# First expert's rows and last expert's sum by one-hot products, and the three passes of each product in another order

## Chip, cores and metric

One core of a Trainium2 chip runs the kernel. The metric is the device time of one launch in microseconds. The median of three runs is 1960.74 us.

## What is computed

Two layers of a decoder trunk on 256 tokens of width 1024, all in float32. The reference, cut to its frame:

```python
for l in range(2):
    h = rmsnorm(x, norm_mix[l])
    ... = split(h @ w_in[l])                      # 5316 columns: three token mixers, and gates
    merged = g0 * (o_a @ w_pa[l]) + g1 * (o_b @ w_pb[l]) + g2 * (o_c @ w_pc[l])
    x = x + merged @ w_out[l]
    x = x + cross_attention(rmsnorm(x), rmsnorm(mem), w_xq[l], w_xkv[l], w_xo[l], ...)
    hf = rmsnorm(x, norm_ffn[l])
    x = x + (swiglu(hf, ...) if l == 0 else moe_swiglu(hf, ...))

def moe_swiglu(t, w_router, w_gu, w_down):        # 8 experts, 1024 -> 2 x 3584 -> 1024
    top_val, top_idx = top_k(t @ w_router, 2)
    gate = sum(one_hot(top_idx) * softmax(top_val))
    return sum(gate[:, e] * swiglu(t, w_gu[e], w_down[e]) for e in range(8))
```

## The kernel before

**Products in three passes.** Every float32 product but those of the gates and the attention is split: the weights w and the activations h each into a rounded high part and a rest, and the product is h_hi w_hi + h_lo w_hi + h_hi w_lo. A weight tile is 1 MB (128 partitions x 2048 floats) in one of three slots `raw`. ACT copies it to `w_hi` (`act_split`, L383; in the expert stage L820), DVE subtracts to get `w_lo` (`dve_split`, L388; L884). Semaphores `hi_done` and `lo_done` count them. Three slots of `w_hi` and `w_lo` go round: the fourth split waits until PE is through with the first (`mm_done`). For the activations ACT writes `hT_hi` (`act_hi`, L490, semaphores such as `mix_H`), DVE `hT_lo` (`dve_lo`, L495, `mix_L`). `pe_products` (L499) runs over the row blocks k of a slot and does all three passes for one k before the next:

```python
pe.matmul(acc, a, wh, start=start and j == 0, stop=False)     # L504
pe.matmul(acc, b, wh, start=False, stop=False)                # L505
ins = pe.matmul(acc, a, wl, start=False, stop=stop and last)  # L506
```

It is called by `pe_block_slot` (L509) for the linears, by `pe_dense` for the dense layer and by `pe_moe_gate_up` and `pe_moe_down` for the experts; each first waits for `lo_done` of its slot and for the low part of the activations. The order of work on each engine is written out by hand, engine by engine. A linear has slots of 4 row blocks x 512 columns, "pa" and "pb" of 2 x 512. Layer by layer come xkv ("mem" is its input), in ("mix"), the mixers, pa, pb, pc, out ("mrg"), xq ("x"), cross attention, xo, and the feed-forward part ("ffn").

**The expert stage.** `dve_router` (L1551) takes the logits, finds the two best experts per token, and PE counts the ranks of the tokens in each expert (L1203 to L1207). From them DVE computes `row_no`, the row that each of a token's two copies has in a list in DRAM, `expert_rows`: 128 rows per expert (L1584), and `n_iter`, the number of blocks of 128 rows, 8 here. DVE normalises x into `xn` (L1683). POOL scatters `xn` into the list by four indirect DMAs (L318), waits for them, and loads block 0 (L321). PE turns the block (`pe_turn_rows`, L754: 8 transposes), ACT and DVE split it (L832, L898), and expert 0 begins. Inside each expert POOL loads the next block, PE turns it after the third chunk, and ACT's output copy `y_sb` of the expert before (L836) is put back in the list by POOL (L329).

An expert is 14 chunks of 256 hidden columns, 3 weight tiles each: two for gate and up (`pe_moe_gate_up`), one for the way down (`pe_moe_down`), the last one for the chunk before. Between the two, PE turns the product silu(gate) * up of the chunk before (L716); ACT makes its high part `aT_hi` (L828), DVE the low one, `aT_lo` (L893, `aT_split`). SP loads tiles six ahead, as DVE frees them. `pe_moe`, `act_moe` and `dve_moe` run expert 0 and 1 apart, then a loop over pairs, whose count each engine reads into a register.

**The end.** The last down product has no chunk around it. ACT: silu, the split of the last tile, `aT_hi`, then the copy of the output (L876 to L880); DVE the same. Then POOL puts the block in DRAM, waits, gathers each token's two rows by four indirect DMAs into `yg` (L335), and DVE adds them to x, times the gates (L937). SP stores each half of the tokens.

## Time and profile before

| | |
|---|---|
| median of three runs | 1960.74 us (1956.84 to 1961.72) |
| the profiled execution: its time, its span | 1955.1 us, 1953.5 us |
| mean granted clock of PE | 0.96 |
| PE busy | 1754.0 us, 90% |
| DVE busy | 1377.2 us, 70% |
| ACT busy | 1059.5 us, 54% |
| POOL busy | 49.8 us, 3% |
| read from HBM | 483.55 MB, 257 GB/s over the span |

Times in the profile are counted from the span's start. PE is the matmul engine, and its busy time is not a measure of its peak; PEld is its weight load. Work is in two halves: up to 950 us the two layers with their mixers, each engine with pauses, and from 953 us on the expert stage.

### The profile page before, as it was taken

How to read it: one execution, taken by the hardware profiler on the slowest of the kernel's cores; microseconds unless marked ns; L12 is line 12 of the kernel's file. 1: busy time of each engine (PE TensorE's matmuls, PEld its weight loads, DVE VectorE, ACT ScalarE, POOL GpSimd, SP SyncE). 2: the span in 40 equal slices, each digit the busy share in tenths (PEclk: the TensorE clock that was granted, in tenths of full speed). 3: DMA queues.
4: the chain of work that ended last, by engine and by line, in shares of the span. 5: the costliest groups of instructions: out<-in, count | busy, mean ns of one | idle time of the engine just before them, and what ended most of it. 6: DMA issues, size and time to landing. Idle time of an engine off the chain costs nothing.

```text
span 1953.5 us, 21775 instructions
## 1 busy us (share of the span) xinstructions
PE 1754.0 (90%) x7553; PEld 1348.9 (69%) x7553; DVE 1377.2 (70%) x1288; ACT 1059.5 (54%) x967; POOL 49.8 (3%) x69
## 2 busy tenths in 40 slices
PE   6796878799989968886499999999999999999995
PEld 5653466688867634665388887888888888888884
DVE  6447467554456464674488888888888888888884
ACT  4212434434343224243377777777777777777773
POOL 2100000000000000000100000000000000000000
PEclk9898989899989989897799999999999999999997
DMA  8821259255435312440699999999999999999993
GB/s 240 266 91 63 82 194 363 103 194 190 175 127 175 109 66 82 178 177 22 233 355 370 376 367 371 371 371 373 367 376 369 366 381 365 376 368 365 382 363 137
DMA packets 74813, 502.80 MB, mean 257 GB/s; under 512 B 8524, under 2 KB 9356, under 8 KB 18320
## 3 DMA queue, kind: packets, MB, share of 16 engines
q1 hardware_dynamic: 65712, 466.55, 62.6%
q0 software_dynamic: 8656, 34.57, 5.7%
q10 hardware_dynamic: 400, 1.08, 0.1%
q8 instruction: 28, 0.46, 0.1%
q14 instruction: 17, 0.14, 0.0%
HBM read 483.55 MB, written 18.61 MB: 257 GB/s over the span
## 4 chain that ended last, share of the span: by engine, by line
PE 76%; DVE 10%; ACT 6%; DMA 3%; issue 2%; DVEq 2%; POOL 0%; ACTq 0%; SPq 0%; POOLq 0%
PE ps L504 23%; PE ps L505 23%; PE ps L506 23%; DMA raw<-in_layer_tiles 3%; PE ps L569 2%; DVE w_lo L388 2%; PE ps L716 1%; ACT scratch L1259 1%; ACT w_hi L383 1%; DVE scratch L1386 1%; DVE st L1357 1%; DVEq L1360 1%; DVE scratch L1436 1%; DVE st L1440 1%; DVE hT_lo L495 1%
## 5 line engine op out<-in xcount | busy, mean ns | idle before, releaser
L504 PE MATMUL ps<-w_hi,hT_hi 128*128 128x512 f32 x1488 | 610.6, 410 | 57.9 <-DVE hT_lo L495 24.1
L505 PE MATMUL ps<-w_hi,hT_lo 128*128 128x512 f32 x1488 | 597.3, 401 | 0.0
L506 PE MATMUL ps<-w_lo,hT_hi 128*128 128x512 f32 x1488 | 596.6, 401 | 0.0
L884 DVE TENSOR_TENSOR w_lo<-raw,w_hi 128x2048 fp32r<-128x2048 f32 x168 | 385.0, 2292 | 69.4 <-ACT w_hi L820 69.4
L884 DVE TENSOR_TENSOR w_lo<-z,w_hi 128x2048 fp32r<-128x2048 f32 x168 | 384.5, 2290 | 51.7 <-ACT w_hi L820 48.6
L504 PEld LDWEIGHTS ps<-w_hi,hT_hi 128*128 128x128 f32 x1488 | 285.1, 192 | 130.4 <-DVE w_lo L388 30.0
L820 ACT ACTIVATE w_hi<-z 128x2048 fp32r<-128x2048 f32 x168 | 321.6, 1915 | 40.6 <-PE ps L506 34.7
L820 ACT ACTIVATE w_hi<-raw 128x2048 fp32r<-128x2048 f32 x168 | 321.0, 1911 | 24.3 <-PE ps L506 24.3
L506 PEld LDWEIGHTS ps<-w_lo,hT_hi 128*128 128x128 f32 x1488 | 285.3, 192 | 68.9
L505 PEld LDWEIGHTS ps<-w_hi,hT_lo 128*128 128x128 f32 x1488 | 285.6, 192 | 62.4
L388 DVE TENSOR_TENSOR w_lo<-raw,w_hi 128x2048 fp32r<-128x2048 f32 (+1 forms) x89 | 194.6, 2194 | 126.9 <-ACT w_hi L383 126.2
L383 ACT ACTIVATE w_hi<-raw 128x2048 fp32r<-128x2048 f32 (+1 forms) x89 | 162.6, 1834 | 199.7 <-PE ps L506 128.9
L504 PE MATMUL ps<-w_hi,aT_hi 128*128 128x512 f32 x536 | 213.6, 398 | 3.5 <-DVE aT_lo L893 2.0
L506 PE MATMUL ps<-w_lo,aT_hi 128*128 128x512 f32 x536 | 212.7, 397 | 0.0
L505 PE MATMUL ps<-w_hi,aT_lo 128*128 128x512 f32 x536 | 212.7, 397 | 0.0
L569 PE MATMUL ps<-raw 128*128 128x512 f32 (+1 forms) x384 | 158.4, 570 | 26.4 <-DVE z L579 26.4
L569 PEld LDWEIGHTS ps<-raw 128*128 128x128 f32 x384 | 72.7, 197 | 107.5 <-issue 107.2
L504 PEld LDWEIGHTS ps<-w_hi,aT_hi 128*128 128x128 f32 x536 | 100.9, 188 | 31.4 <-issue 5.5
L506 PEld LDWEIGHTS ps<-w_lo,aT_hi 128*128 128x128 f32 x536 | 101.1, 189 | 24.5
L505 PEld LDWEIGHTS ps<-w_hi,aT_lo 128*128 128x128 f32 x536 | 101.0, 188 | 23.7
L828 ACT ACTIVATE aT_hi<-ps 128x256 fp32r<-128x256 f32 x112 | 43.2, 385 | 107.9 <-PE ps L716 107.9
L824 ACT ACTIVATE headsT<-ps 128x256 f32<-128x256 f32 x112 | 42.9, 383 | 65.4 <-PE ps L506 65.4
(235 smaller groups left out, 1015.8 us busy)
## 6 DMA issues: line engine op xcount, KB each, us to landing
z<-in_moe_tiles SPq DMA_DIRECT2D x168, 1024.0 KB, 4.9
raw<-in_moe_tiles SPq DMA_DIRECT2D x168, 1024.0 KB, 4.8
raw<-in_layer_tiles SPq DMA_DIRECT2D x68, 1024.0 KB, 4.9
raw<-in_dense_tiles SPq DMA_DIRECT2D x33, 1024.0 KB, 4.8
rows_of_experts<-z POOLq DMA_DIRECT2D x1, 8704.0 KB, 44.2
z<-in_b_gate POOLq DMA_DIRECT2D x4, 1536.0 KB, 11.4
z<-rows_of_experts POOLq DMA_DIRECT2D x9, 512.0 KB, 8.2
raw<-in_layer_tiles SPq DMA_DIRECT2D x8, 512.0 KB, 3.9
```

What stands on the lines that cost most here:

```text
L383: act.activation(w_hi[:, ring, 0:width], raw[:, ring, 0:width], ACT.Copy).then_inc(sem("hi_done"), 1)
L388: v.tensor_tensor(w_lo[:, ring, 0:width], raw[:, ring, 0:width], w_hi[:, ring, 0:width].bitcast(F32), ALU.subtract).then_inc(sem("lo_done" ...
L495: v.tensor_tensor(hT_lo[:, ks, :], src[:, ks, :], hT_hi[:, ks, :].bitcast(F32), ALU.subtract) \
L504: pe.matmul(acc, a, wh, start=start and j == 0, stop=False)
L505: pe.matmul(acc, b, wh, start=False, stop=False)
L506: ins = pe.matmul(acc, a, wl, start=False, stop=stop and last)
L569: ins = pe.matmul(ps[:, LIN + i, 0:n], gate_x(l)[:, kk, i * P:(i + 1) * P], w[:, k, :], start=kk == 0, stop=kk == KC - 1)
L716: ins = pe.transpose(ps[:, 6, f * P:(f + 1) * P], a_sb[:, 0, f * P:(f + 1) * P], ident)
L820: act.activation(w_hi[:, ring, :], moe_raw(p), ACT.Copy).then_inc(sem("hi_done"), 1)
L824: act.activation(silu_sb[:, 0, :], ps[:, bank, 0:FC], ACT.Silu).then_inc(sem("silu"), 1)
L828: act.activation(aT_hi[:, :, 0:P], psA(1), ACT.Copy).then_inc(sem("aT_hi"), 1)
L884: v.tensor_tensor(w_lo[:, ring, :], moe_raw(p), w_hi[:, ring, :].bitcast(F32), ALU.subtract) \
```

## The change

1. `pe_products` does the high-high matmuls of all row blocks first, then the low-high ones, then high-low. The wait before it asks for the high parts (`hi_done`, `..._H`, `aT_hi`); those for the low part of the activations (`x_lo`) and of the weights (`w_lo_v`) stand between the passes, for the first column tile of a slot.
2. The first block is not read back from DRAM. DVE makes `first_hot`, 128 tokens x 128 rows, from the smaller of a token's two row numbers, and PE multiplies `xn` by it (L803 of the new file), which gives the turned rows at once. `xn` is x times the gain, made by DVE before the router, then scaled by ACT. The scatter of all rows stays.
3. The last block's output is not put in DRAM. `dve_last` makes `last_hot` between the second and third expert, PE turns it, ACT copies it. At the end PE multiplies `y_sb` by it, half by half, and DVE adds the result to x times the gate. The rows of the other experts are gathered during the last expert, and POOL scales and adds them. The list's padding block is loaded only after the last put has landed.
4. At the end, the split of the last tile stands ahead of the last silu, and the output is stored in quarters.

The diff, cut:

```diff
+            for n in range(2 * TT):
+                h, i = n // TT, n % TT
+                sp.wait_ge(sem("x_final"), n + 1)
+                sp.dma_start(out[0, i * P:(i + 1) * P, h * NB:(h + 1) * NB], x_sb[:, i, h * NB:(h + 1) * NB]) \
+                    .then_inc(sem("stored"), 16)
+            sp.wait_ge(sem("stored"), 16 * 2 * TT)
...
-            load_rows(pool, 0)
             pool.wait_ge(sem("routed"), 1)
             n_it = pool.value_load(n_iter[0:1, 0:1], min_val=N_EXP, max_val=2 * N_EXP)
-            def turn_rows(m, done):
+            with pool.Fori(1, n_it) as m:
 
                 pool.wait_ge(sem("rows_T"), m)
                 load_rows(pool, m)
                 pool.wait_ge(sem("y_sb"), m)
-                pool.dma_start(expert_rows[bass.ds(m * P - P, P), :], y_sb).then_inc(sem(done), 16)
-            with pool.Fori(1, n_it) as m:
-                turn_rows(m, "rows_put")
-            turn_rows(n_it, "last_put")
-            pool.wait_ge(sem("last_put"), 16)
+                pool.dma_start(expert_rows[bass.ds(m * P - P, P), :], y_sb).then_inc(sem("rows_put"), 16)
+            pool.wait_ge(sem("rows_T"), n_it)
+            pool.wait_ge(sem("rows_put"), n_it * 16)
+            load_rows(pool, n_it)
+
             for k in range(2 * TT):
                 pool.indirect_dma_start(yg[:, k, :], None, expert_rows, bass.IndirectOffsetOnAxis(row_no[:, k:k + 1], 0)) \
                     .then_inc(sem(f"y_back{k}"), 16)
+            pool.wait_ge(sem("g_split"), 1)
+            for k in range(2 * TT):
+                j, i = k // TT, k % TT
+                pool.wait_ge(sem(f"y_back{k}"), 16)
+                if j:
+                    pool.wait_ge(sem("x_part"), i + 1)
+                pool.tensor_scalar(yg[:, k, :], yg[:, k, :], g_other[:, j, i:i + 1], None, ALU.mult)
+                pool.drain()
+                pool.tensor_tensor(x_sb[:, i, :], x_sb[:, i, :], yg[:, k, :], ALU.add).then_inc(sem("x_part"), 1)
...
-        def pe_products(pe, acc, hk, wk, start, stop, hi=hT_hi, lo=hT_lo):
-
-            for j, ((k, cols), (wh, wl)) in enumerate(zip(hk, wk)):
-                a, b = hi[:, k, cols], lo[:, k, cols]
-                last = j == len(hk) - 1
-                pe.matmul(acc, a, wh, start=start and j == 0, stop=False)
-                pe.matmul(acc, b, wh, start=False, stop=False)
-                ins = pe.matmul(acc, a, wl, start=False, stop=stop and last)
+        def pe_products(pe, acc, hk, wk, start, stop, hi=hT_hi, lo=hT_lo, x_lo=None, w_lo_v=None):
+
+            for j, ((k, cols), (wh, _)) in enumerate(zip(hk, wk)):
+                pe.matmul(acc, hi[:, k, cols], wh, start=start and j == 0, stop=False)
+            if x_lo is not None:
+                pe.wait_ge(sem(x_lo[0]), x_lo[1])
+            for (k, cols), (wh, _) in zip(hk, wk):
+                pe.matmul(acc, lo[:, k, cols], wh, start=False, stop=False)
+            if w_lo_v is not None:
+                pe.wait_ge(sem("lo_done"), w_lo_v)
+            for j, ((k, cols), (_, wl)) in enumerate(zip(hk, wk)):
+                ins = pe.matmul(acc, hi[:, k, cols], wl, start=False, stop=stop and j == len(hk) - 1)
             return ins
 
-        def pe_block_slot(pe, ring, kcs, n, k0, lo_v, first, final, blk_v):
-
-            pe.wait_ge(sem("lo_done"), lo_v)
+        def pe_block_slot(pe, ring, kcs, n, k0, lo_v, first, final, blk_v, x_lo=None):
+
+            pe.wait_ge(sem("hi_done"), lo_v)
...
+                                  x_lo=x_lo if i == 0 else None, w_lo_v=lo_v if i == 0 else None)
...
+                    x_lo = None
                     if h_ready and b == b0:
-                        pe.wait_ge(sem(h_ready), 2 * l + h + 1)
-                    pe_block_slot(pe, place[ss_], kcs, n, k0 + 4 * h, split_no(ss_) + 1, h == 0, h == per - 1, evs)
+                        pe.wait_ge(sem(h_ready + "_H"), 2 * l + h + 1)
+                        x_lo = (h_ready + "_L", 2 * l + h + 1)
...
-                pe.wait_ge(sem("aT_split"), c + 1)
+                pe.wait_ge(sem("hi_done"), s + (1 - N_GATE))
+                pe.wait_ge(sem("aT_hi"), c + 1)
...
-            pe_turn_rows(pe, 0)
+            pe.wait_ge(sem("first_hot"), 1)
+            pe.wait_ge(sem("xn_rows"), 1)
+            for k in range(KC):
+                for i in range(TT):
+                    ins = pe.matmul(psG[:, k, :], xn[:, i, k * P:(k + 1) * P], first_hot[:, i, :],
+                                    start=i == 0, stop=i == TT - 1)
+            ins.then_inc(sem("rows_T"), 1)
             for par in range(2):
                 pe_expert(pe, 0, par)
+            pe.wait_ge(sem("last_hot"), 1)
+            for i in range(TT):
+                ins = pe.transpose(ps[:, 7, i * P:(i + 1) * P], last_hot[:, i, :], ident)
+            ins.then_inc(sem("last_T"), 1)
...
+            lo_v, aT_v = n_pair * (2 * MOE) + SPL0, n_pair * (2 * N_MOE) + N_DENSE
+            pe.wait_ge(sem("hi_done"), lo_v)
+            pe.wait_ge(sem("aT_hi"), aT_v)
...
+                pe_products(pe, ps[:, h, :], [(f, slice(0, P)) for f in range(2)],
+                            [(wh[:, f, cols], wl[:, f, cols]) for f in range(2)], False, True, hi=aT_hi, lo=aT_lo,
+                            x_lo=("aT_split", aT_v) if h == 0 else None, w_lo_v=lo_v if h == 0 else None) \
+                    .then_inc(sem("last_y"), 1)
+            pe.wait_ge(sem("last_to_token"), 1)
+            for h in range(2):
+                pe.wait_ge(sem("last_y_sb"), h + 1)
+                for i in range(TT):
+                    pe.matmul(ps[:, LAST[h][i], :], last_to_token[:, i * P:(i + 1) * P], y_sb[:, h * NB:(h + 1) * NB],
+                              start=True, stop=True).then_inc(sem("spread"), 1)
...
+            act.wait_ge(sem("top_two"), 1)
+            act.activation(g2[:, 0:2], g2[:, 0:2], ACT.Exp).then_inc(sem("gate_exp"), 1)
+            act.wait_ge(sem("last_T"), 1)
+            act.activation(last_to_token, ps[:, 7, 0:2 * P], ACT.Copy).then_inc(sem("last_to_token"), 1)
             act.wait_ge(sem("routed"), 1)
             n_pair = act.value_load(n_iter[0:1, 1:2], min_val=N_EXP // 2, max_val=N_EXP)
             with act.Fori(1, n_pair) as ip:
                 for par in range(2):
                     act_expert(act, ip, par)
+            act_moe_split(act, 2, moe_ring(0), n_pair * (MOE // 3 * 16), n_pair * (2 * MOE) + (MOE0 - 3))
...
             act_silu(act, 5, n_pair * (2 * MOE) + (MOE0 - 2))
-            act_moe_split(act, 2, moe_ring(0), n_pair * (MOE // 3 * 16), n_pair * (2 * MOE) + (MOE0 - 3))
...
-            act_y(act, n_pair * (2 * MOE) + MOE0)
+            for h in range(2):
+                act.wait_ge(sem("last_y"), h + 1)
+                act.activation(y_sb[:, h * NB:(h + 1) * NB], ps[:, h, :], ACT.Copy).then_inc(sem("last_y_sb"), 1)
...
+            dve_last(v)
...
+            dve_moe_split(v, 2, moe_ring(0), n_pair * (2 * MOE) + SPL0)
             dve_gated(v, 5, n_pair * (2 * N_MOE) + N_DENSE)
-            dve_moe_split(v, 2, moe_ring(0), n_pair * (2 * MOE) + SPL0)
...
-                for j in range(2):
-                    v.wait_ge(sem(f"y_back{j * TT + i}"), 16)
-                    ins = v.scalar_tensor_tensor(x_sb[:, i, :], yg[:, j * TT + i, :], g2[:, 4 + 2 * j + i:5 + 2 * j + i],
-                                                 x_sb[:, i, :], ALU.mult, ALU.add)
-                    v.drain()
-                v.drain().then_inc(sem("x_final"), 1)
+            v.wait_ge(sem("x_part"), 2 * TT)
+            for n in range(2 * TT):
+                h, i = n // TT, n % TT
+                dst = x_sb[:, i, h * NB:(h + 1) * NB]
+                v.wait_ge(sem("spread"), n + 1)
+                v.scalar_tensor_tensor(dst, ps[:, LAST[h][i], :], slot[:, i:i + 1], dst, ALU.mult, ALU.add) \
+                    .then_inc(sem("x_final"), 1)
...
+                    act.wait_ge(sem("ffn_rs"), l + 1)
+                    for i in range(TT):
+                        ins = act.activation(xn[:, i, :], xn[:, i, :], ACT.Copy, scale=norm_rs[:, 6 + i:7 + i])
+                    ins.then_inc(sem("xn_rows"), 1)
...
+            dve_newton(v, "ffn", L - 1, norm_rs[:, 6:8]).then_inc(sem("ffn_rs"), 1)
...
+            v.tensor_tensor(slot, row_f[:, 0, :], row_f[:, 1, :], ALU.min)
+            v.drain()
+            for i in range(TT):
+                ins = v.tensor_scalar(first_hot[:, i, :], iota, slot[:, i:i + 1], None, ALU.is_equal)
+            ins.then_inc(sem("first_hot"), 1)
...
+        def dve_last(v):
+
+            v.tensor_scalar(last0, n_f[:, 2:3], float(P), -float(P), ALU.mult, ALU.add)
+            v.drain()
+            v.tensor_scalar(from_last, row_f, last0, None, ALU.subtract)
+            v.drain()
+            v.tensor_tensor(slot, from_last[:, 0, :], from_last[:, 1, :], ALU.max)
+            v.tensor_scalar(in_last, from_last, 0.0, None, ALU.is_ge)
+            v.drain()
+            for i in range(TT):
+                ins = v.tensor_scalar(last_hot[:, i, :], iota, slot[:, i:i + 1], None, ALU.is_equal)
+            ins.then_inc(sem("last_hot"), 1)
...
+            v.tensor_tensor(g_last, g, in_last, ALU.mult)
+            v.drain()
+            v.tensor_tensor(g_other, g, g_last, ALU.subtract).then_inc(sem("g_split"), 1)
+            v.tensor_tensor(slot, g_last[:, 0, :], g_last[:, 1, :], ALU.add)
...
-                    dve_newton(v, "ffn", l, norm_rs[:, 6:8])
-                    v.drain()
                     v.wait_ge(sem("gain_row"), 16)
                     for i in range(TT):
-                        ins = v.scalar_tensor_tensor(xn[:, i, :], x_sb[:, i, :], norm_rs[:, 6 + i:7 + i], gain_row,
-                                                     ALU.mult, ALU.mult)
-                    ins.then_inc(sem("xn_rows"), 1)
+                        v.tensor_tensor(xn[:, i, :], x_sb[:, i, :], gain_row, ALU.mult)
```

`pe_moe_down`, `pe_moe_gate_up` and the functions of `pe_dense` take the new waits in the same way as `pe_block_slot`.

**Place 1: PE, the down product of a chunk in the expert loop.** `aT_hi`, `aT_lo` are the turned activations, and the waits are semaphores. Before:

```order
L504 MATMUL ps<-w_hi,aT_hi 128x512 [waits aT_split,lo_done]
L505 MATMUL ps<-w_hi,aT_lo 128x512
L506 MATMUL ps<-w_lo,aT_hi 128x512
L504 MATMUL ps<-w_hi,aT_hi 128x512
L505 MATMUL ps<-w_hi,aT_lo 128x512
L506 MATMUL ps<-w_lo,aT_hi 128x512
L504 MATMUL ps<-w_hi,aT_hi 128x512
L505 MATMUL ps<-w_hi,aT_lo 128x512
L506 MATMUL ps<-w_lo,aT_hi 128x512
```

After the change:

```order
L512 MATMUL ps<-w_hi,aT_hi 128x512 [waits aT_hi,hi_done]
L512 MATMUL ps<-w_hi,aT_hi 128x512
L516 MATMUL ps<-w_hi,aT_lo 128x512 [waits aT_split]
L516 MATMUL ps<-w_hi,aT_lo 128x512
L520 MATMUL ps<-w_lo,aT_hi 128x512 [waits lo_done]
L520 MATMUL ps<-w_lo,aT_hi 128x512
L512 MATMUL ps<-w_hi,aT_hi 128x512 x2
L516 MATMUL ps<-w_hi,aT_lo 128x512 x2
L520 MATMUL ps<-w_lo,aT_hi 128x512 x2
```

Matmuls of one pass now stand together, two in each half of the columns, where the three passes alternated; the waits for the two low parts have moved behind two and four matmuls.

**Place 2: ACT, from the last turn of the second expert to the first split of the third.** L865 (before: L820) is the copy to `w_hi`, L873 (L828) `aT_hi`. Before:

```order
L828 ACTIVATE aT_hi<-ps 128x2x128 [waits aT_turned]
L813 REGISTER_ALU
L813 COMPARE_AND_BRANCH
L872 TENSOR_LOAD n_iter [waits routed]
L872 ISA x2
L873 UNCONDITIONAL_BRANCH
L873 ISA
L819 ISA [waits moe_full0]
L820 ACTIVATE w_hi<-z 128x2048 [waits mm_done]
```

After:

```order
L873 ACTIVATE aT_hi<-ps 128x2x128 [waits aT_turned]
L858 REGISTER_ALU
L858 COMPARE_AND_BRANCH
L917 ACT_TABLE_LOAD
L917 ACTIVATE headsT<-headsT 128x2 [waits top_two]
L919 ACTIVATE scratch<-ps 128x256 [waits last_T]
L921 TENSOR_LOAD n_iter [waits routed]
L921 ISA x2
L922 UNCONDITIONAL_BRANCH
L922 ISA
L864 ISA [waits moe_full0]
L865 ACT_TABLE_LOAD
```

Between them stand the exponential of the gates with its table, and a copy of what PE turns at `last_T`. On PE these two turns stand behind the last down product of the second expert:

```order
L520 MATMUL ps<-w_lo,aT_hi 128x512 x2
L794 REGISTER_ALU
L794 COMPARE_AND_BRANCH
L810 MATMUL ps<-consts,scratch 128x128 [waits last_hot]
L810 MATMUL ps<-consts,scratch 128x128
L813 TENSOR_LOAD n_iter [waits routed]
L813 ISA x2
```

Before, nothing of ACT's stood there but the register's load.

**Place 3: ACT at the end.** Before:

```order
L823 ISA
L824 ACTIVATE headsT<-ps 128x256 [waits mm_done]
L818 REGISTER_ALU
L819 REGISTER_ALU [waits moe_full2]
L820 ACTIVATE w_hi<-z 128x2048 [waits mm_done]
L827 ISA
L828 ACTIVATE aT_hi<-ps 128x2x128 [waits aT_turned]
```

After:

```order
L863 REGISTER_ALU
L864 ISA [waits moe_full2]
L865 ACTIVATE w_hi<-z 128x2048 [waits mm_done]
L868 REGISTER_ALU
L869 ACTIVATE headsT<-ps 128x256 [waits mm_done]
L872 ISA
L873 ACTIVATE aT_hi<-ps 128x2x128 [waits aT_turned]
```

The split of the last tile (`moe_full2`) has moved ahead of the silu (L869, before L824).

## Rows read from the trace of the kernel before

**Rows 1.** Windows, expert stage: us, busy by engine, clock of PE, DMA share, GB/s.

```profile
1100.00:1400.00 300.00, 300.00 (x1335) 241.10 (x1334) 262.62 (x177) 222.79 (x177) 2.13 (x4) 1.00 0.96 371
```

**Rows 2.** Timeline (start, duration), PE from one tile to the next.

```profile
1900.37 0.40 PE L506 MATMUL ps<-w_lo,aT_hi 128*128 128x512 f32 x1
1900.37 0.19 PEld L504 LDWEIGHTS ps<-w_hi,hT_hi 128*128 128x128 f32 x1
1900.61 0.40 PE L504 MATMUL ps<-w_hi,hT_hi 128*128 128x512 f32 x1
```

**Rows 3.** Waits of PE: total us, times, longest.

```profile
PE ps L504 <- DVE hT_lo L495: 24.1, 11, 3.6
...
PE ps L504 <- DVE w_lo L388: 8.5, 4, 2.2
...
PE ps L504 <- DVE w_lo L884: 1.6, 1, 1.6
```

**Rows 4.** Timeline, the start of the first expert; in brackets idle before, releaser.

```profile
917.71 2.48 DVE L1683 SCALAR_TENSOR_TENSOR scratch<-x_sb,st,z 128x1024 f32<-128x1024 f32 x2
...
925.72 0.17 DVE L1584 CAST row_no<-headsT 128x4 uint32<-128x4 f32 x1
...
945.18 0.59 POOL L310 DMA_DIRECT2D z<-rows_of_experts  x1 [10.71 <-DMA rows_of_experts<-scratch,row_no]
...
948.68 1.97 PE L758 MATMUL ps<-consts,z 128*128 128x128 f32 x8 [24.08 <-DMA z<-rows_of_experts]
950.69 1.02 ACT L832 ACTIVATE hT_hi<-ps 128x1024 fp32r<-128x1024 f32 x1 [24.23 <-PE ps L758]
...
951.74 1.22 DVE L898 TENSOR_TENSOR hT_lo<-ps,hT_hi 128x1024 fp32r<-128x1024 f32 x1 [19.36 <-ACT hT_hi L832]
...
953.02 0.80 PE L504 MATMUL ps<-w_hi,hT_hi 128*128 128x512 f32 x1 [2.37 <-DVE hT_lo L898]
```

**Rows 5.** Timeline, the end.

```profile
1926.04 2.29 DVE L884 TENSOR_TENSOR w_lo<-z,w_hi 128x2048 fp32r<-128x2048 f32 x1 [1.38 <-ACT w_hi L820]
...
1926.42 0.38 PE L716 MATMUL ps<-consts,headsT 128*128 128x128 f32 x2
...
1928.82 0.48 PE L504 MATMUL ps<-w_hi,aT_hi 128*128 128x512 f32 x1 [2.01 <-DVE aT_lo L893]
...
1933.44 1.02 ACT L836 ACTIVATE z<-ps 128x1024 f32<-128x1024 f32 x1 [6.22 <-PE ps L506]
...
1947.73 2.64 DVE L937 SCALAR_TENSOR_TENSOR x_sb<-scratch,headsT,x_sb 128x1024 f32<-128x1024 f32 x2 [0.17 <-issue]
```

**Rows 6.** Timeline, PE in "pa" of the first layer.

```profile
257.17 0.69 PE L504 MATMUL ps<-w_hi,hT_hi 128*128 128x512 f32 x1 [2.10 <-DVE w_lo L388]
257.66 0.63 PE L505 MATMUL ps<-w_hi,hT_lo 128*128 128x512 f32 x1
258.08 0.63 PE L506 MATMUL ps<-w_lo,hT_hi 128*128 128x512 f32 x1
```

**Rows 7.** Timeline, PE with whole float32 operands.

```profile
163.62 1.06 PE L1060 MATMUL ps<-scratch,consts 128*128 128x128 f32 x4
...
190.85 3.70 PE L569 MATMUL ps<-raw 128*128 128x512 f32 x8
```

**Rows 8.** Timeline, ACT's table load; ACT and PE from second to third expert.

```profile
953.53 1.28 ACT L824 ACT_TABLE_LOAD   x1
...
1192.62 1.92 ACT L820 ACTIVATE w_hi<-z 128x2048 fp32r<-128x2048 f32 x1 [0.78 <-issue]
...
1196.91 0.50 PE L504 MATMUL ps<-w_hi,hT_hi 128*128 128x512 f32 x1
```

**Rows 9.** DMA issues: count, KB each, us from issue to landing, in the expert stage.

```profile
rows_of_experts<-z POOLq DMA_DIRECT2D x2, 512.0 KB, 6.7
z<-rows_of_experts POOLq DMA_DIRECT2D x2, 512.0 KB, 8.2
```

**Rows 10.** Timeline, POOL in the first layer.

```profile
288.24 3.84 POOL L281 MEMSET z<- 128x4488 f32 x1 [152.47 <-DVE scratch L1487]
```

90 lines of the change are left out of this document (50 added, 40 removed).

## The prediction

> **What bounds the kernel now.** I read four views: the windows, the waits of PE, the timeline of the three places that the change touches, and the groups by line. The profiled execution took 1955.1 us, 5.6 us under the median of the runs (1960.74); all sums are made against it, and the difference is carried over to the median at the end.
>
> Half of the span, from 953 us on, is the expert stage: 8 experts, 14 chunks each, 3 weight tiles a chunk. There PE is never idle: 300 us of a 300 us window [rows 1]. Its products follow each other every 0.233 us, also from the last of one weight tile to the first of the next, which has a wait before it [rows 2]. A chunk of 36 products and two turns (the transposes, about 0.11 us each) takes 8.61 us. Here only fewer or faster products would help, and the change has the same number. DVE and ACT have 12% and 26% idle in it, DMA is at 0.96.
>
> What can be won lies outside. Of the first half the reader should see the waits of PE for the low part of an operand [rows 3], and two holes: the start of the first expert, where PE stands for 24.1 us until the rows come back from DRAM [rows 4], and the end, where nothing but one expert's output is written out, gathered and added [rows 5].
>
> **Part 1, high-high passes first.** Each product of a slot now asks for the high parts alone, does its high-high matmuls, then waits for the low part of the activations, then for that of the weights. PE reaches the wait with 4 matmuls done (2 where the slot has 2 row blocks, and 8 where the weights are the late part). The pause itself stays, so each such wait gives at most the matmuls put ahead of it: 4 x 0.233 = 0.93 us at the high clock, 4 x 0.427 = 1.7 at the low one [rows 6], and about DVE's own part at most, 1.22 us for 1024 columns [rows 4] and 2.29 for 2048 [rows 5].
> - activations of "mem", two layers, at the low clock, where DVE still makes the weights' low half as well: 2 x 1.7 = 3.4
> - "mix", two layers: 0.9 and 1.2; "out" and "x", two layers: 4 x 0.93; "ffn" 0.93: 6.8. With "mem" these are the waits for hT_lo, 24.1 us in 11 waits, two of which (the start of "xo") keep theirs.
> - the four waits for w_lo in "pa" and "pb", 8.5 us together [rows 3], with 2 high-high and 2 low-high matmuls ahead each: 4 x 1.0 = 4.0
> - the end of the dense layer, aT_lo, 2 matmuls: 0.5.
>
> That is 14.7 us. In the expert stage one wait is left, 1.6 us for w_lo in the first chunk [rows 3]; 8 matmuls (1.87 us) now cover it: 1.6.
> The clock: after a wait of 2.1 us eight matmuls come 0.427 us apart [rows 6], so PE is at the lower of its two levels (1.2 GHz); each such stretch costs 8 x 0.194 = 1.6 us. Nine such stretches stand behind a wait that becomes shorter or is broken in two. None need go (0), all may (14). I take 4, nearer the low end: waits of about 2 us have a fall behind them [rows 5, 6], and no row here tells how short is short enough. Part 1 in all: 20.3.
>
> **Part 2, the first expert's rows from SBUF.** Before [rows 4] the two normalising operations end and the router begins at 920.1, row numbers are there at 925.9, the expert's first matmul is at 953.0. Now those two (2.48 us from 917.71) leave the path: DVE multiplies x by the gain alone, from 914.2 on, and the router starts at 916.9, when the logits land. That is 3.2 us earlier: row arithmetic ends at 922.5, plus a minimum and two 128-column comparisons, about 0.7: 923.2. ACT has scaled the rows by then (Newton steps 920.0, two of 1.05: 922.0). PE does 16 fp32 matmuls of 128 columns. Four of these took 1.06 us at the low clock with the last one's tail [rows 7], 0.215 each: 16 x 0.215 = 3.4, and 0.3 until ACT sees them: 926.9. ACT makes the high part in 1.02 [rows 4], and PE starts at 928.0 with 4 matmuls; DVE, which has two weight splits first (to 928.5), adds the low part by 929.7. So the start moves from 953.0 to 928.0: **25.0**. The four row scatters and the second expert's load now run beside the first chunks: the scatters had landed 19.3 us after the row numbers (the load of 945.18), so now near 943, the load near 950, and PE asks for these rows after 8 tiles, at 953. Costed at nothing; if that cover is gone PE stands for the difference.
>
> **Part 3, the end.** Before [rows 5]: turn 1926.4, last down product starts 1928.8, since ACT's silu stood ahead of its last split and DVE's too; PE ends at 1933.4, half of it at the low clock; then ACT's copy, the store, the gather, four additions until 1950.4, the output stored by 1953.5. Now the split runs in the idle of ACT from 1921.4 (it needs a slot that PE freed at 1920.7): high part 1923.4, low 1925.7, gated product 1926.1, in time for the turn. PE starts at 1927.3 on aT_hi, 12 x 0.233: 1930.1. The gap is 0.6 us in place of 2.0, so I expect the high clock to hold. The first half of y is copied meanwhile (0.6). Four fp32 matmuls of 512 columns, 0.46 each (eight in 3.70 [rows 7]): 1931.9, and DVE adds four halves of 0.75 behind them: 1933.7. With the same 3.1 us from last addition to end: 1936.8, a gain of **16.7**; at the low clock from 1929 on it would be 13.5.
>
> **What it costs.** (a) Between the second and third expert ACT now waits for PE: the exponential of the gates with its table load (1.28 [rows 8]), then "last_T", two turns that PE does after the last down product. Before, ACT had made the next tile's high part by then: it began at 1192.62 and was done 2.4 us before PE wanted it at 1196.91 [rows 8]. Now: PE free at 1196.85, turns seen 0.4 later, copy 0.38, register load 0.78, a table load again 1.28, split 1.92: PE stands until 1201.6, 4.5 us. The low halves then come from DVE one after another (2.29 each, three and two short ones before aT_lo), while PE wants aT_lo after 24.5 matmuls: another 2. Together -6.5. The loop's two further table loads per pair of experts hide in ACT's idle quarter; if that is gone, 1.5 us for each of 3 pairs.
> (b) In the last expert POOL waits for the seventh expert's put to land before it loads the padding block that PE still turns: put at 10.1 us into the expert, 6.7 to land, then 8.2 [rows 9]: 25.5, when PE wants it at 25.9. The gather of 2 MB follows at once. Bounds 0 and 8; I take -1.5, near the lower end, since tiles are asked for six ahead.
> (c) POOL's eight operations on 128x1024, and DVE's 15 small ones between experts two and three (inside the stall of (a)): 0.5.
>
> Sum: 20.3 + 25.0 + 16.7 - 6.5 - 2.0 = **53.5**. Own time 1901.6; carried to the median, 1907.
>
> **A rule against this change.** The nearest row for POOL's arithmetic is the clearing of z, 4488 columns in 3.84 us [rows 10], so 0.88 us for 1024 with one input, and I double it for two: 4 x (0.88 + 1.76) = 10.6 us. No two-input DVE operation ran from SBUF beside it, so what it does to DVE is not in the trace; bounds are 0 and the 10.6 whole.
> The Trainium skill, page "GPSIMD Engine Reference", section "Key points", says that POOL shares its SBUF interfaces with VectorE and contends with DVE instructions that have two SBUF inputs. w_lo is exactly such an instruction.
>
> **Rivals.**
> 1. POOL holds DVE up. All 10.6 us stand in DVE's way; its 12% idle over some 30 us takes 3.6, and PE waits 7: 1914. This is the page's rule as named above. 12%.
> 2. The early start starves. The rows of expert two, or tiles behind the scatters, come later than PE asks, with PE standing 5 to 12 us and its clock falling: 1907 + 10 = 1917. For: DMA at 0.96 in the stage. Against: 6 tiles lie ready, and the first 8 take PE 24 us. 12%.
> 3. The clock gives more: all low stretches go, and (a) costs 4: 1907 - 10 - 2.5 = 1894. 12%.
> 4. Slower than before: the new wait in the middle of a product keeps PE from loading the next weights ahead. Place: the wait for lo_done before the third pass, 336 tiles in the expert stage alone. Price: one exposed load, 0.19 us each [rows 2], 64 us: 1971. It decides from 0.16 us per tile. Against: the waits that stand at each tile's start now cost 0.00 [rows 2]. 3%.
> 5. The change does less than it says: the first-pass matmuls just move a wait, nothing downstream comes earlier since the loads of weight tiles set the pace; part 1 gives 5: 1922. 6%.
>
> **How the numbers follow.** Forecast 55%: 1907, with its own bounds 1900 to 1915. The range takes in rivals 1, 2 and part of 3 and 5: 1896 to 1922. A measurement tells 0.3% (6 us) from no change. Only rival 4 is no gain: faster 0.96, same 0.01, slower 0.03.
>
> **What would show it.** L512 replaces L504 in PE's waits with the same pauses, now split over L512, L516 and L520, about 15 us less in total. First L512 of the first expert 25 us plus part 1 earlier, and no L779 wait in front of it. A wait of 4 to 5 us of PE for ACT w_hi at the third expert, once. From PE's last down product to the end 7 to 8 us in place of 20.1. Wrong if the chunk in the expert stage is not 8.61 us any more (rival 4), if DVE's w_lo lengthens beside POOL (rival 1), or if PE waits for DMA at L779 (rival 2).

## The result, and the profile after

The changed kernel took 1916.48 us (median of 4 runs, 1909.52 to 1917.71) beside 1961.23 for the kernel before on the same chip: ratio 0.977 [0.974, 0.979], 44.8 us less where 53.5 were forecast. The time lies in the range, 9.5 us above 1907. The profiled execution has a span of 1914.1 us, 39.4 less than that of before. In the four later measurements of this document the kernel before had medians of 1955.0 to 1956.9 us, near its profiled execution (1955.1), so 1961.23 may lie some 5 us high and 39.4 may be the better size of the gain. From the page of the profile:

```profile
span 1914.1 us, 21886 instructions
PE 1762.0 (92%) x7587; PEld 1350.6 (71%) x7587; DVE 1384.1 (72%) x1300; ACT 1070.5 (56%) x978; POOL 82.9 (4%) x75
```

The waits of PE (total us, times, longest), which answer to [rows 3]:

```profile
PE ps L512 <- DVE z L596: 13.1, 3, 11.4
...
PE ps L512 <- ACT hT_hi L500: 8.8, 9, 1.8
...
PE ps L516 <- DVE aT_lo L944: 5.3, 7, 1.7
...
PE ps L512 <- ACT w_hi L865: 4.3, 1, 4.3
...
PE ps L520 <- DVE w_lo L398: 3.0, 4, 1.2
PE ps L512 <- DVE hT_lo L505: 2.8, 2, 1.4
...
PE ps L779 <- DMA z<-rows_of_experts: 2.6, 1, 2.6
...
PE ps L512 <- ACT w_hi L393: 1.6, 3, 0.7
```

The waits for the parts of operands fell: hT_lo from 24.1 us to 2.8 here and 1.3 in L516, with 8.8 for hT_hi in its place, and w_lo from 8.5 to 3.0, with 1.3 of the 1.6 for w_hi in its place, 15.4 in all. Other waits ahead of the router grew by part of that: "z" by 2.7, evacuations into scratch ahead of L512 by 2.3, x_sb by 1.9; others fell. The stretch up to the router, first before, then after (the second number is its length, then PE's time at work; 0.95 is the granted clock):

```profile
0.00:912.80 912.80, 768.96 (x3183) 556.49 (x3184) 511.54 (x677) 328.78 (x384) 30.11 (x44) 0.95 0.45 155
```
```profile
0.00:900.08 900.08, 769.34 (x3184) 552.45 (x3184) 511.13 (x676) 328.70 (x384) 30.17 (x44) 0.95 0.45 157
```

So PE stands 143.8 us before the router in the old kernel and 130.7 in the new one, 13.1 less, and its time at work is 769.0 and 769.3. Three waits of the expert stage are new or have grown: 5.3 us for aT_lo, 4.3 for w_hi and 2.6 for the padding rows, where PE had stood for nothing over long stretches [rows 1].

The timeline of PE from router to first product, which answers to [rows 4]:

```profile
900.08 3.71 PE L1260 MATMUL ps<-w_router,scratch 128*128 128x8 f32 x32 [0.20 <-ACT scratch L1395]
...
910.29 5.67 PE L803 MATMUL ps<-scratch 128*128 128x128 f32 x32 [1.89 <-DVE scratch L1650]
917.08 1.20 PE L512 MATMUL ps<-w_hi,hT_hi 128*128 128x512 f32 x4 [1.11 <-ACT hT_hi L877]
```

The router starts 12.7 us earlier (912.80 before), the first product 35.9 earlier: 12.7 from part 1, 23.2 from part 2. The end, which answers to [rows 5]:

```profile
1903.39 0.38 PE L735 MATMUL ps<-consts,headsT 128*128 128x128 f32 x2
1904.34 0.70 PE L512 MATMUL ps<-w_hi,aT_hi 128*128 128x512 f32 x2 [0.57 <-ACT aT_hi L873]
...
1907.20 3.59 PE L835 MATMUL ps<-z,scratch 128*128 128x512 f32 x8
1908.34 3.25 DVE L991 SCALAR_TENSOR_TENSOR x_sb<-ps,headsT,x_sb 128x512 f32<-128x512 f32 x4 [3.69 <-PE ps L835]
```

From the start of the last down product to the end it is 9.7 us (24.7 before), and the gap ahead of it 0.57 in place of 2.01.

Between the first product and the last down product the stage grew from 975.8 to 987.3 us. To see where, read one turn (L735, L716 before) to the next. Before, a chunk is 8.61 us, and 9.49 where the rows of the next expert are turned. Now four places differ:

| turns | before | after | more |
|---|---|---|---|
| start of the third expert (27th and 28th) | 8.78, 8.63 | 14.94, 9.13 | 6.7 |
| end of a pair of experts, twice | 8.61 | 9.28 | 1.4 |
| padding rows turned (at 1793.7) | 9.49 | 13.57 | 4.1 |
| three chunks from 1824.5 on | 8.61 | 10.58, 9.74, 9.67 | 4.2 |

### The profile page after: what moved, and what is told of

It reads as the page before. It is cut to its first block, busy times and chain, and to the rows that moved or that the text cites. A ratio compares the mean times of both kernels' runs of the same rounds, so it can differ in the third digit from the quotient of the medians.

```text
span 1914.1 us, 21886 instructions
## 1 busy us (share of the span) xinstructions
PE 1762.0 (92%) x7587; PEld 1350.6 (71%) x7587; DVE 1384.1 (72%) x1300; ACT 1070.5 (56%) x978; POOL 82.9 (4%) x75
## 4 chain that ended last, share of the span: by engine, by line
PE 73%; DVE 11%; ACT 7%; DMA 4%; issue 3%; DVEq 2%; ACTq 0%; SPq 0%; POOLq 0%
PE ps L516 22%; PE ps L520 22%; PE ps L512 22%; DMA raw<-in_layer_tiles 3%; DVE w_lo L398 2%; PE ps L586 2%; DVE w_lo L935 1%; ACT w_hi L393 1%; PE ps L735 1%; ACT scratch L1321 1%; DVE scratch L1450 1%; DVE st L1421 1%; ACT w_hi L865 1%; DVEq L1424 1%; DVE scratch L1500 1%
## 5 line engine op out<-in xcount | busy, mean ns | idle before, releaser
L512 PE MATMUL ps<-w_hi,hT_hi 128*128 128x512 f32 x1488 | 427.2, 408 | 45.2 <-DVE z L596 13.1
L935 DVE TENSOR_TENSOR w_lo<-raw,w_hi 128x2048 fp32r<-128x2048 f32 x168 | 391.1, 2329 | 64.3 <-ACT w_hi L865 64.3
L516 PE MATMUL ps<-w_hi,hT_lo 128*128 128x512 f32 x1488 | 414.8, 400 | 1.8 <-DVE hT_lo L505 1.3
L520 PE MATMUL ps<-w_lo,hT_hi 128*128 128x512 f32 x1488 | 412.7, 399 | 3.0 <-DVE w_lo L398 3.0
L512 PEld LDWEIGHTS ps<-w_hi,hT_hi 128*128 128x128 f32 x1488 | 271.7, 191 | 108.5 <-issue 22.7
L865 ACT ACTIVATE w_hi<-z 128x2048 fp32r<-128x2048 f32 x168 | 321.3, 1915 | 40.7 <-PE ps L520 35.9
L865 ACT ACTIVATE w_hi<-raw 128x2048 fp32r<-128x2048 f32 x168 | 320.9, 1911 | 25.5 <-PE ps L520 25.5
L516 PEld LDWEIGHTS ps<-w_hi,hT_lo 128*128 128x128 f32 x1488 | 282.6, 190 | 73.5 <-DVE hT_lo L505 5.2
L586 PE MATMUL ps<-raw 128*128 128x512 f32 (+1 forms) x384 | 162.0, 581 | 28.1 <-DVE z L596 28.1
L516 PE MATMUL ps<-w_hi,aT_lo 128*128 128x512 f32 x536 | 169.2, 397 | 5.3 <-DVE aT_lo L944 5.3
L512 PE MATMUL ps<-w_hi,aT_hi 128*128 128x512 f32 x536 | 168.5, 396 | 1.3 <-ACT aT_hi L702 0.8
L520 PE MATMUL ps<-w_lo,aT_hi 128*128 128x512 f32 x536 | 168.4, 396 | 0.0
L586 PEld LDWEIGHTS ps<-raw 128*128 128x128 f32 x384 | 74.0, 200 | 111.6 <-issue 111.4
L516 PEld LDWEIGHTS ps<-w_hi,aT_lo 128*128 128x128 f32 x536 | 100.1, 188 | 32.4 <-DVE aT_lo L944 8.3
L512 PEld LDWEIGHTS ps<-w_hi,aT_hi 128*128 128x128 f32 x536 | 100.5, 188 | 25.9 <-issue 1.8
L873 ACT ACTIVATE aT_hi<-ps 128x256 fp32r<-128x256 f32 x112 | 43.2, 386 | 106.6 <-PE ps L735 106.6
L869 ACT ACTIVATE headsT<-ps 128x256 f32<-128x256 f32 x112 | 43.2, 385 | 57.6 <-PE ps L520 57.5
## 6 DMA issues: line engine op xcount, KB each, us to landing
z<-in_b_gate POOLq DMA_DIRECT2D x4, 1536.0 KB, 11.1
```

The lines of the kernel that those rows point to most:

```text
L512: pe.matmul(acc, hi[:, k, cols], wh, start=start and j == 0, stop=False)
L516: pe.matmul(acc, lo[:, k, cols], wh, start=False, stop=False)
L520: ins = pe.matmul(acc, hi[:, k, cols], wl, start=False, stop=stop and j == len(hk) - 1)
L586: ins = pe.matmul(ps[:, LIN + i, 0:n], gate_x(l)[:, kk, i * P:(i + 1) * P], w[:, k, :], start=kk == 0, stop=kk == KC - 1)
L865: act.activation(w_hi[:, ring, :], moe_raw(p), ACT.Copy).then_inc(sem("hi_done"), 1)
L869: act.activation(silu_sb[:, 0, :], ps[:, bank, 0:FC], ACT.Silu).then_inc(sem("silu"), 1)
```

## The experiments

Where no repeated runs are given, an experiment was one execution beside the kernel before, and is read by its turns: they agree within 0.03 us between executions where nothing was changed, while the start of the router wanders by 2.5 us (899.9 to 902.4 in nine executions with the new order).

**1. Part 1 alone.** The kernel before with the new `pe_products` and its split waits:

```diff
-            for j, ((k, cols), (wh, wl)) in enumerate(zip(hk, wk)):
-                pe.matmul(acc, a, wh, ...); pe.matmul(acc, b, wh, ...); pe.matmul(acc, a, wl, ...)
+            (all a*wh); wait x_lo; (all b*wh); wait w_lo; (all a*wl)
```

> The kernel before with nothing but the new order of the passes and its split waits. Theory (the waits for the low parts went as forecast, but waits that stood behind them took back about half): the router starts near 900.1 instead of 912.8, 12.7 us earlier, about 1.5 us more at the first expert's start, and the expert stage's chunks stay at 8.61; the run is 12 to 15 us below the kernel before (ratio 0.993). Rival A (the other two parts, through POOL's queue and the SBUF-resident rows, ate the rest of the gain): 18 to 21 us below, router start near 894. Rival B (most of the early gain came from luck in the clock): 4 to 6 us below.

1939.4 us (4 runs, 1938.1 to 1940.2) beside 1956.0, ratio 0.991 [0.989, 0.993], 17 us less. Its PE:

```profile
902.39 3.71 PE L1207 MATMUL ps<-w_router,scratch 128*128 128x8 f32 x32 [0.20 <-ACT scratch L1342]
938.22 1.97 PE L769 MATMUL ps<-consts,z 128*128 128x128 f32 x8 [24.03 <-DMA z<-rows_of_experts]
...
1914.38 0.70 PE L502 MATMUL ps<-w_hi,aT_hi 128*128 128x512 f32 x2 [0.56 <-ACT aT_hi L837]
1915.74 0.73 PE L506 MATMUL ps<-w_hi,aT_lo 128*128 128x512 f32 x2 [0.65 <-DVE aT_lo L902]
```

In its profile 15.1 us are gone: 10.4 by the router, 2.6 from there to the last turn, and 2.1 behind it, where the gap is shorter and the last products stay at the high clock (0.233 us apart; before, more than half of them were 0.43 apart). Rival A is out: the other parts did not eat part 1's early gain, it never was 18. At this end the forecast had given part 1 nothing.

**2. The new order with the old waits.** In `pe_products` both waits stand ahead of the first pass.

```diff
+            wait x_lo; wait w_lo
             (all a*wh)
-            wait x_lo
             (all b*wh)
-            wait w_lo
             (all a*wl)
```

> The changed kernel with both waits for low parts moved ahead of the first pass of each product; the order of the matmuls stays the new one. Theory (what gains is that the first pass runs while the low parts are made, not the order as such): the router starts near 912 instead of 900, the whole is 12 to 15 us slower than the changed kernel, near 1930. Rival A (the order itself, hi after hi, helps by the clock or the weight loads): under 6 us slower, near 1921. Rival B (mid-product waits cost something of their own in every chunk): the expert chunks get shorter than 8.61 here.

1937.4 us (4 runs, 1935.2 to 1941.9), ratio 0.991 [0.988, 0.993]; the changed kernel's is 0.977. More is lost than expected: the router starts at 915.77, 15.7 later than in the changed kernel and 3 later even than in the kernel before, and one wait of the stage grew:

```profile
915.77 3.71 PE L1260 MATMUL ps<-w_router,scratch 128*128 128x8 f32 x32 [0.20 <-ACT scratch L1395]
...
1183.84 2.04 PE L516 MATMUL ps<-w_hi,hT_hi 128*128 128x512 f32 x4 [6.72 <-DVE w_lo L935]
```

PE stands 141.5 us before the router here, 11 more than in the changed kernel, and is at work for 5.0 more. So the order as such brings nothing to the time: what gains is that the first pass runs while the low parts are made. At the third expert the split waits also soften the new stall: 4.30 us in the changed kernel, 6.72 here. Rival A is out. Rival B too: no chunk is shorter, and those next to an expert's change take 8.82.

**3. Without POOL's arithmetic.** The eight operations and `v.wait_ge(sem("x_part"), 2 * TT)` are taken out of the changed kernel.

> The changed kernel without POOL's eight arithmetic operations and without VectorE's wait for them: the additions of the rows of all experts but the last are left out of the output. Theory (POOL beside VectorE stretches the splits of the last chunks): the chunks that began at 1824.5, 1833 and 1845 and took 1.95, 1.14 and 1.06 us more than 8.61 fall back to 8.61, 4.2 us less, and the low splits of that stretch fall from 3.2 to 3.6 us to 2.3. Rival (the gathers' transfers and low clock do it): the three chunks stay at 9.7 to 10.6, 0 to 1 us less.

The three chunks are back at 8.61 and DVE's splits at 2.29 us, and PE's waits for aT_lo in the stage fall from 5.3 us to 1.9; the one execution took 1908.9 us. Changed kernel, DVE and POOL at the same time:

```profile
1822.21 7.29 DVE L935 TENSOR_TENSOR w_lo<-raw,w_hi 128x2048 fp32r<-128x2048 f32 x2
...
1832.88 6.36 DVE L935 TENSOR_TENSOR w_lo<-z,w_hi 128x2048 fp32r<-128x2048 f32 x2
```
```profile
1819.78 4.88 POOL L344 TENSOR_SCALAR scratch<-scratch,headsT 128x1024 f32<-128x1024 f32 x1
1824.82 2.52 POOL L346 TENSOR_TENSOR x_sb<-x_sb,scratch 128x1024 f32<-128x1024 f32 x1 [0.15 <-issue]
1827.33 4.89 POOL L344 TENSOR_SCALAR scratch<-scratch,headsT 128x1024 f32<-128x1024 f32 x1
1832.36 2.52 POOL L346 TENSOR_TENSOR x_sb<-x_sb,scratch 128x1024 f32<-128x1024 f32 x1
```

Two splits take 4.58 us when alone. The pair from 1822.21 takes 7.29, which is 2.7 more; 2.2 of that are in its second split, which shares 2.3 us with the addition, and 0.6 in the first. The pair from 1832.88 takes 1.8 more and shares 2.0 us with the next addition. It looks as if DVE stood for about as long as it shares with POOL's addition, and hardly for its multiplication. Run 4 tests that.

**4. POOL with one-input operations only.** Each addition is replaced by a second multiplication:

```diff
                 pool.tensor_scalar(yg[:, k, :], yg[:, k, :], g_other[:, j, i:i + 1], None, ALU.mult)
                 pool.drain()
-                pool.tensor_tensor(x_sb[:, i, :], x_sb[:, i, :], yg[:, k, :], ALU.add).then_inc(sem("x_part"), 1)
+                pool.tensor_scalar(yg[:, k, :], yg[:, k, :], g_other[:, j, i:i + 1], None, ALU.mult)
```

> The changed kernel with each of POOL's four tensor_tensor additions replaced by a second tensor_scalar on the same rows: the other experts' rows are left out of the output. Theory A (POOL beside VectorE slows it whatever POOL does): the turns of the last expert are stretched as before, 3 to 4.2 us in all, and low splits of 128x2048 there take 3 to 3.6 us instead of 2.29. Theory B (only POOL's operations with two SBUF inputs get in VectorE's way): the stretch falls to 0 to 1.5 us.

Theory B. All chunks from 1824 on take 8.61, though POOL is busy longer than before. DVE, then POOL, of this run:

```profile
1827.23 5.08 DVE L933 TENSOR_TENSOR w_lo<-z,w_hi 128x2048 fp32r<-128x2048 f32 x2
1832.94 2.41 DVE L933 TENSOR_TENSOR w_lo<-raw,w_hi 128x2048 fp32r<-128x2048 f32 x1 [0.30 <-ACT w_hi L863]
```
```profile
1826.14 3.55 POOL L344 TENSOR_SCALAR scratch<-scratch,headsT 128x1024 f32<-128x1024 f32 x1 [0.17 <-issue]
1829.67 5.27 POOL L342 TENSOR_SCALAR scratch<-scratch,headsT 128x1024 f32<-128x1024 f32 x1
```

Beside it a single split takes 2.28 to 2.88 us in place of 2.29, which DVE's idle 12% hides. The Trainium skill, page "GPSIMD Engine Reference", section "Key points", names DVE instructions with two SBUF inputs as those that contend. The trace agrees with that half: in the changed kernel, DVE's operations that read PSUM and one SBUF tile take 0.41 us beside POOL's additions (at 1832.54 and 1842.20) as they do elsewhere. The other half is POOL's own operation: with one input it costs a split at most 0.6 us, with two it costs up to 2.2.

**5. The padding rows ahead of the put.**

```diff
             pool.wait_ge(sem("rows_T"), n_it)
-            pool.wait_ge(sem("rows_put"), n_it * 16)
             load_rows(pool, n_it)
+            pool.wait_ge(sem("rows_put"), n_it * 16)
+            (a load of four bytes behind that wait)
```

> The changed kernel with the load of the last expert's rows ahead of the wait for the last put (one four-byte load behind that wait is added). Theory (the load waited for the put that it does not need): the transposes of the last expert's rows wait 0 instead of 2.6 us, the chunk at 1793.7 takes 8.6 to 9.5 instead of 13.6, 2.6 to 4.1 us less in all. Rival (TensorE was late there for the clock and the gathers): the wait goes and the chunk stays above 11, at most 2 us less.

The wait is gone and the turn takes 9.48: 4.1 less. But the executions of other kernels, which keep the order of the change here, have anything from 9.48 to 16.79. POOL's load, with its wait for the put in brackets, in the changed kernel, in run 7 and in run 6:

```profile
1793.42 0.53 POOL L312 DMA_DIRECT2D z<-rows_of_experts  x1 [8.58 <-DMA rows_of_experts<-z]
```
```profile
1786.15 0.53 POOL L312 DMA_DIRECT2D z<-rows_of_experts  x1 [6.93 <-DMA rows_of_experts<-z]
```
```profile
1790.87 0.53 POOL L312 DMA_DIRECT2D z<-rows_of_experts  x1 [11.05 <-DMA rows_of_experts<-z]
```

Their turns take 13.57, 9.48 and 16.79. Over the eight traces with this order the turn follows the wait: four with 6.8 to 6.9 us have 9.48, the others 11.14 (8.3 us), 13.57 (8.6), 15.53 (9.4) and 16.79 (11.1). So the put's landing decides, and it varies where no code near it differs: with 6.9 us the load is in time, with 11.1 PE waits 4.33 us and then works at the low clock. The edit takes this lottery away; its worth is 0 to 7 us an execution, and 4.1 was one draw.

**6. The copy of the last expert's one-hots late.** ScalarE's two lines move to the tail:

```diff
             act.activation(g2[:, 0:2], g2[:, 0:2], ACT.Exp).then_inc(sem("gate_exp"), 1)
-            act.wait_ge(sem("last_T"), 1)
-            act.activation(last_to_token, ps[:, 7, 0:2 * P], ACT.Copy).then_inc(sem("last_to_token"), 1)
...
+            act.wait_ge(sem("last_T"), 1)
+            act.activation(last_to_token, ps[:, 7, 0:2 * P], ACT.Copy).then_inc(sem("last_to_token"), 1)
             act.wait_ge(sem("rows_put"), n_pair * 32)
```

> The changed kernel with ScalarE's wait for the last expert's transposed one-hots, and the copy of them, moved from between the second and the third expert to the tail, ahead of the last expert's output. Theory (ScalarE is held there until TensorE comes round, and its splits are late for the third expert): the wait for ACT w_hi at the third expert, 4.3 us, falls under 1 us and the turn that took 14.94 us takes 8.6 to 10.5, 4.5 to 6.3 us less in all; the turns of 9.28 at each pair's end (two of them) stay. Rival (the exponential's table load and the late tokens hold ScalarE up as well): the turn stays above 12, at most 3 us less.

The wait is gone; the turns are 8.97 and 10.23 in place of 14.94 and 9.13, 4.9 us less. Left are three table loads, and the two pair ends at 9.29. (The whole, 1913.4 us, hides that: its draw at the padding rows was the 16.79 above.) ACT in the changed kernel:

```profile
1153.45 1.28 ACT L917 ACT_TABLE_LOAD   x1
1154.74 0.20 ACT L917 ACTIVATE headsT<-headsT 128x2 f32<-128x2 f32 x1
1158.85 0.38 ACT L919 ACTIVATE scratch<-ps 128x256 f32<-128x256 f32 x1 [3.90 <-PE ps L810]
1159.85 1.28 ACT L865 ACT_TABLE_LOAD   x1 [0.62 <-issue]
1161.15 1.91 ACT L865 ACTIVATE w_hi<-z 128x2048 fp32r<-128x2048 f32 x1
```

PE wants that tile at 1158.8, and gets it at 1163.1:

```profile
1163.11 1.90 PE L512 MATMUL ps<-w_hi,hT_hi 128*128 128x512 f32 x4 [4.30 <-ACT w_hi L865]
1164.81 1.91 PE L516 MATMUL ps<-w_hi,hT_lo 128*128 128x512 f32 x4
1166.51 1.20 PE L520 MATMUL ps<-w_lo,hT_hi 128*128 128x512 f32 x4
...
1171.46 0.72 PE L516 MATMUL ps<-w_hi,aT_lo 128*128 128x512 f32 x2 [0.25 <-DVE aT_lo L944]
```

The first eight matmuls behind the wait are 0.425 us apart, at the low clock, which is 1.5 us; the wait for aT_lo is 0.25.

**7. And the exponential early,** in the first expert's hook, behind the high parts of its rows:

```diff
                 if what == "first rows":
                     act_rows_hi(act, 1, 0)
+                    act.wait_ge(sem("top_two"), 1)
+                    act.activation(g2[:, 0:2], g2[:, 0:2], ACT.Exp).then_inc(sem("gate_exp"), 1)
```

> As the run with the late copy, and the gates' exponential moved into the first expert, behind its first high parts of rows. Theory (the exponential and its table load are what is left at the third expert): that turn falls to 8.6, 0.5 to 1.5 us less than with the late copy alone, and the first expert gets 0 to 1.3 us longer, since it has slack in its low-clock start. Rival (the table load now delays the first expert's activation): the first turns get over 1.3 us longer and nothing is won against the late copy alone.

The turns are 8.81 and 9.09, 1.3 less than in run 6 and 6.2 less than in the change, and the pair ends fall to 8.61 as well, 1.4 that I had not expected. ACT of the changed kernel, at the end of a pair:

```profile
1403.34 1.28 ACT L865 ACT_TABLE_LOAD   x1 [0.23 <-issue]
1406.57 1.28 ACT L869 ACT_TABLE_LOAD   x1
```

These two stand at the head of each round of the loop, though nothing in a round needs another table, and in run 7 ACT loads none in the whole stage after the first expert. It reads as if the loop's head had to hold for the entry from the exponential as well. The first turns did not change. The run took 1904.9 us.

**8. The write of distance rows later,** to see what swallows part 1's first gain.

```diff
-            pool.wait_ge(sem("mm_done"), 2)
+            pool.wait_ge(sem("mm_done"), 5)
             pool.dma_start(scratch_dram, dist_rows.unsqueeze(1).to_broadcast([H, P, 3 * P])) \
```

> The changed kernel with POOL's write of the 2.3 MB of distance rows held until the fifth weight tile's matmuls instead of the second. Theory (the weight tiles of the first layer land behind that write, so that what part 1 gains in the first 60 us is waited away at 68.5): the wait there, 11.4 us, falls by 4 us or more, the raw tile's landing falls from 13.6 us towards 5 to 8, and the first slot of the attention starts up to 8 us earlier; if the bias is then late there, a wait for it shows instead. Rival (the waits there are VectorE's, behind the head norms): the wait stays within 1 us of 11.4 and everything after it where it was.

First row the changed kernel, then this run (its row ends with its window at 80 us):

```profile
68.52 2.05 PE L512 MATMUL ps<-w_hi,hT_hi 128*128 128x512 f32 x4 [11.40 <-DVE z L596]
```
```profile
79.02 1.19 PE L512 MATMUL ps<-w_hi,hT_hi 128*128 128x512 f32 x2 [11.23 <-DVE z L596]
```

The wait moved with the write, undiminished, and the float32 products that follow the layer's weight tiles start at 135.6 (136.1 in the changed kernel, 135.2 in the one before). By its numbers the rival came, the expected gain was not there; yet the cause is not the rival's, as runs 9 and 10 show: the write costs the weight tiles the same at both places. The releaser's name misled here: DVE evacuates late because the weights were late. In ACT's rows of the changed kernel the cause is named (63.47, waiting 12.38 us for raw<-in_layer_tiles).

**9 and 10. Both kernels without the write.** The write and the loads are left out, POOL sets the bias to zero.

> The changed kernel without the 2.3 MB write of the distance rows and the twelve loads that read them back; POOL sets the bias to zero instead, so the position bias is left out. Theory (in the first layer the transfers, that write among them, set the pace, and part 1's first gain is lost to them): the wait of 11.4 us at 68.5 is gone, the first dense head of the first layer (the products that start at 136.1 in the changed kernel) starts by 128 or earlier, and the router starts 8 to 12 us before 900.1. Rival (TensorE would have waited there for evacuation anyway): under 3 us earlier.

> The kernel before with the same edit: no write of the distance rows, no loads of them, the bias set to zero. Theory (part 1's gain in the first layer shows once the write is out of its way): this kernel gains less from the edit than the changed one, since its own waits for low parts stand in the way; at 135.2 it gains 4 to 8 us, and the distance between the two kernels at the first layer's products grows from minus 0.9 (the changed one is even later) to 3 us or more in favour of the changed one. Rival (the new order has nothing to gain in the first layer): the distance stays under 1 us.

The changed kernel took 1903.0 us (4 runs), ratio 0.972 [0.970, 0.974], the kernel before 1946.0 (4 runs), 0.995 [0.993, 0.997]. The wait of 11.4 us is gone in both. Where the first layer's weight tiles end (136.07 and 135.21 with the write), first the changed kernel, then the one before (both rows end with their window at 124 us):

```profile
121.33 3.12 PE L582 MATMUL ps<-raw 128*128 128x512 f32 x4 [3.71 <-DVE z L592]
```
```profile
122.65 1.78 PE L565 MATMUL ps<-raw 128*128 128x512 f32 x3 [3.70 <-DVE z L575]
```

The write costs each of them 13 to 15 us there. The distance at this place goes from 0.9 us against the changed kernel to 1.3 in its favour: right in sign, under the 3 us expected. So up to this place the transfers took some 2 us of part 1's gain. The low clock then takes what is left: at 200 us 16 matmuls (L1168) took 3.47 us in the changed kernel and 1.95 in the other (L1106), and the two were level again. Behind it the distance grows: the router starts at 889.5 and 905.4, 15.9 us apart where it was 12.7 with the write. That is one execution of each, and the router's start wanders by 2.5 us.

**11. All mended.** Edits 5, 6 and 7, and the other experts' rows multiplied and added by VectorE in the tail:

```diff
-            v.wait_ge(sem("x_part"), 2 * TT)
+            for j in range(2):
+                for i in range(TT):
+                    v.wait_ge(sem(f"y_back{j * TT + i}"), 16)
+                    v.scalar_tensor_tensor(x_sb[:, i, :], yg[:, j * TT + i, :], g_other[:, j, i:i + 1],
+                                           x_sb[:, i, :], ALU.mult, ALU.add)
```

> The changed kernel with the copy late, the exponential early, the last block's load ahead of the put, and the other experts' rows multiplied and added by VectorE at the very end (four operations) instead of by POOL's eight during the last expert. Theory: 4.1 us from the load, 6.7 from ScalarE at the third expert, 4.2 from VectorE's splits, less 4 x 1.4 us of VectorE before the last sums of which the last product hides most: 12 to 15 us below the changed kernel, 1902 on the clock of the first measurement, ratio 0.970 to the kernel before. Rival (the additions at the end lie bare, or the earlier turns come back elsewhere): 6 to 10 us below, ratio 0.973.

1901.9 us (5 runs, 1901.1 to 1902.5), ratio 0.972 [0.971, 0.974], against 0.977 [0.974, 0.979] for the change: 8 us or so less by the ratios, nearer the rival, though the two profiled executions are 13.1 apart, as in the theory. In the profile the turns behave: 961.6 us from first to last in place of 977.5, 15.9 less. Given back are 1.2 us at the end, since the additions are not all covered:

```profile
1890.24 5.37 DVE L982 SCALAR_TENSOR_TENSOR x_sb<-scratch,headsT,x_sb 128x1024 f32<-128x1024 f32 x4
1895.68 2.73 DVE L989 SCALAR_TENSOR_TENSOR x_sb<-ps,headsT,x_sb 128x512 f32<-128x512 f32 x4
```

and 1.4 by a router that began later in this execution. The two ratios come from different measurements, and the kernel before was slower in the first of them, so I compare them no closer.

**12. And a quarter of the write.** Thirty-two copies of each row suffice if the rows are read back in four blocks:

```diff
-            pool.dma_start(scratch_dram, dist_rows.unsqueeze(1).to_broadcast([H, P, 3 * P])) \
+            pool.dma_start(scratch_dram, dist_rows.unsqueeze(1).to_broadcast([H, 32, 3 * P])) \
...
+                for b in range(4):
+                    src = bass.AP(scratch_dram.tensor, h * 32 * 3 * P + P - 1 - 32 * b,
+                                  [[3 * P - 1, 32], [32 * 3 * P, n], [1, 2 * P]])
```

> The run with all four edits, and the write of distance rows cut to a quarter: 32 copies of each head's row instead of 128 (0.6 MB instead of 2.3), read back by 16 loads of 32 partitions each instead of 12 of 128. Theory (without that write both kernels reached the same place of the first layer 12.6 and 14.7 us earlier): the first layer's products at 136.1 start 8 to 12 us earlier and the ratio to the kernel before falls from 0.9725 to 0.967 to 0.969, some 1893 on the clock of the first measurement. Rival (the many small reads cost as much, or later waits absorb the gain): 0.971 to 0.973.

1896.0 us (5 runs, 1893.2 to 1899.1) beside 1956.9, ratio 0.969 [0.967, 0.970]: as expected. The wait of 11.4 us is 4.22, at 71.93, and the products of 136.1 start at 127.12. It leaves nothing out, and is faster than both kernels.

## Why the prediction was right, and where it was off

Against the profiles, 39.4 of 53.5 us came. By its steps:

| step | forecast | in the profile |
|---|---|---|
| Part 1, to the router | 18.7 | 12.7 |
| Part 1, first chunks of the stage | 1.6 | 2.2 |
| Part 2 | 25.0 | 23.2 |
| Part 3 | 16.7 | 16.4 |
| (a) ACT waits between experts two and three | -6.5 | -6.7 |
| (a) the pairs' table loads | 0 | -1.4 |
| (b) padding rows | -1.5 | -4.1 |
| (c) POOL beside DVE | -0.5 | -4.2 |

They add up to 38.1; 1.3 us lie in small differences of other turns. The profiled execution of before was 6.1 us under the median that it is compared with (1961.23) and that of the change 0.8, so by medians 44.8 came. The forecast had the gains of parts 2 and 3 in the right places, but the sum was 14 us too large against the profiles. The measured 1916.5 lies 1.5 us outside the forecast's own bounds (1900 to 1915), and in the range only through the width that it had for the rivals.

- **Parts 2 and 3 were right**, in place and size. In part 2 one term was miscounted: a float32 matmul stands in the trace as two instructions, so [rows 7]'s x4 are two calls and 16 calls take 5.67 us, not 3.4; the spreads likewise 3.59, not 1.85. In part 3 luck made up for the miscount: the last addition ends 0.8 us behind the last spread where 1.8 were allowed, and the span 2.5 behind that in place of 3.1. Of part 3's gain, run 1 shows, part 1 alone gives 2.1.
- **(a) was right in its main term**: 4.3 us of wait for w_hi against 4.5 foretold, and runs 6 and 7 take it away. Its second term, 2 us until aT_lo, had the right size by luck: that wait was 0.25, and 1.5 were the low clock behind the stall (run 6). That the pairs' table loads hide was wrong by 0.7 a pair (run 7).
- **Part 1 failed in the step "The clock: ... I take 4".** The waits gave 13.1 us of 14.7: the terms by name were even too small (16.1 came, with 0.7 for aT_lo), but other waits next in line took back 3.0 net. The clock gave nothing in sum, though it did where the forecast looked for it. In "pa", where [rows 6] has its matmuls 0.427 us apart behind the wait, they are now 0.233 apart:

```profile
256.87 0.73 PE L512 MATMUL ps<-w_hi,hT_hi 128*128 128x512 f32 x2 [0.60 <-ACT w_hi L393]
...
258.95 0.63 PE L512 MATMUL ps<-w_hi,hT_hi 128*128 128x512 f32 x2
259.42 0.63 PE L516 MATMUL ps<-w_hi,hT_lo 128*128 128x512 f32 x2
```

  Counted from one start to the next, waits left out, the split products of 512 columns up to the router took 502.7 us before and 497.6 after, and 94 and 55 of them went at the low clock. But the products of whole float32 operands took 3.6 us more (L586, L569 before) and the remaining matmuls 1.9 more, and the stretches of low granted clock up to the router add up to 95.6 us in both kernels. The low clock moved from the one kind of matmul to the other. In the nine traces with the new order, split waits and the write, the time at work is 765.2 to 770.6, beside 769.0 in the one trace of the kernel before. So the bound of 0 was the right value here; why the low stretches come to the same sum stays open, and without the write (runs 9 and 10, one trace each) they did not: 78.5 us against 95.6, and 765.2 at work against 772.3. Transfers took some 2 us in the first layer (runs 8 to 10); rival 5, that the loads of tiles set the pace, held there only.
- **(b) was priced from one landing of the put, 6.7 us [rows 9].** The landing ranges from 6.8 to 11.1 us over the executions, and the cost from 0 to 7.3. The bounds, 0 and 8, were right.
- **(c) was priced at next to nothing where rival 1 had the mechanism.** I doubled POOL's memset for two inputs (1.76 us; it is 2.5) and took DVE's idle time as cover. For one input I took 0.88; the multiplications take 2.9 to 7.0, and all eight operations 30.2 us, not 10.6. That the four additions alone make 10.6 is luck. The rule that the prediction took from the Trainium skill (page "GPSIMD Engine Reference", section "Key points") pointed right; runs 3 and 4 show that of POOL's operations the additions matter. The chance of 12% for rival 1 was too small for a rule that fitted word for word; its price, 7 us of PE, too high by 3 (4.2 in the change, 3.1 to 3.9 in other traces that keep these operations).
- Rivals 2, 3 and 4 did not come. Rows for the second expert were there in time (no wait at L779 before the last), and plain chunks stayed 8.61 us with the low parts' waits in the middle of each tile's products, so the mid-product waits cost nothing.

## What to carry to other kernels

Splitting an operand's wait by its first use is free, but credit it with the gap to the next thing that is late, not with the whole of the work moved ahead. Before an in-order engine waits for a rare event (a copy, a put) between two stages of a tight pipeline, ask for how long its steady work stands behind it: moving such a step to where the engine is idle anyway gave back 6.2 of the 6.7 us here (runs 6 and 7). A helper engine with idle time is not free when its operation reads two SBUF operands beside another engine that does too; measure a pair of turns with and without it.

## What the runs showed of the hardware

- POOL's tensor_tensor of 128x1024 float32 (2.52 us) holds up a two-input tensor_tensor of DVE for about the time that they share (2.2 us of 2.3, 1.9 of 2.0); POOL's tensor_scalar of the same size costs a split of 2.29 us between 0 and 0.6, and itself takes 2.9 to 7.0 us.
- A put of 512 KB beside the weight stream of the expert stage (DMA share 0.96 [rows 1]) kept POOL waiting 6.8 to 11.1 us for its landing in eight traces with the same code at that place.
- A 2.3 MB write from 12 partitions, 37 us from issue to landing, keeps PE waiting 11 us for its weight tiles at either of two places (11.4 and 11.2, gone without the write); with a quarter of it (10 us to land) the wait is 4.2.
- A float32 matmul is recorded as two instructions, 32 records for 16 calls (L803), 8 for 4 (L835), but a float32 transpose as one: 8 for 8 (L758 in [rows 4]).
- An exponential ahead of a loop brought two table loads of 1.28 us into each of its rounds, 0.7 us of PE's time at the end of each pair (runs 6 and 7).
